# Overflow experts' weights asked for by halves and waited for one by one, and retention's first panels asked for after the gate/up products

## The reference, cut to what matters

```python
for i in range(DEPTH):                       # DEPTH = 4
    kind = i % 3                             # 0 attention, 1 pooling, 2 retention
    mp, ms = adaln(c_ctx, w_ada[i]), adaln(c, w_ada[i])
    x = x + gate * mixer[kind](modulate(rmsnorm(x)))
    x = x + gate * moe(modulate(rmsnorm(x)))

def moe(t):                                  # top-1 of 4 groups, top-2 of 4 experts in it
    hg = einsum('td,edf->tef', t, w_gate)    # (16 experts, 1024, 256)
    hu = einsum('td,edf->tef', t, w_up)      # (16 experts, 1024, 256)
    act = silu(hg) * hu * gates[:, :, None]
    return einsum('tef,efd->td', act, w_down)   # (16 experts, 256, 1024)

def retention(h):                            # layer 2 only
    p = h @ w_in                             # (1024, 6144): q, k, v, gate of 8 heads
```

## Time and profile before

| | |
|---|---|
| median of 3 executions | 1488.9 us (1486.45 to 1489.36) |
| the profiled execution | 1489.63 us |
| its span, first to last instruction | 1487.7 us |
| PE busy | 1390.4 us (93%) |
| DVE busy | 729.7 us (49%) |
| mean granted TensorE clock | 0.982 of full |
| mean DMA rate | 279 GB/s |

### The profile page before, as it was taken

One profiled execution on the slowest core, in us unless ns is written; L12 is line 12 of the kernel. 1 busy time (PEld: TensorE's weight loads), 2 busy tenths in 40 slices (PEclk: granted clock), 3 DMA queues, 4 the chain that ended last, 5 costly groups with the idle time before them and its releaser, 6 DMA issues. The chain is left out here.

```text
span 1487.7 us, 18189 instructions
## 1 busy us (share of the span) xinstructions
PE 1390.4 (93%) x6741; PEld 745.7 (50%) x6741; DVE 729.7 (49%) x1869; ACT 309.3 (21%) x697; POOL 92.2 (6%) x102
## 2 busy tenths in 40 slices
PE   5998898999699999899999999999996999999996
PEld 2334544544376443556666666446442446565442
DVE  1254303644527544666666666216542557146444
ACT  2104404110143100511111111013100305241111
POOL 0000011000220001000000000010000110110003
PEclk9999999999899999999999999999998999999998
DMA  9988976899678997745555555247999841047995
GB/s 381 401 325 350 420 284 269 345 424 416 255 287 333 418 423 272 269 127 176 182 183 172 167 172 209 84 199 286 405 422 404 329 179 64 6 165 294 423 423 204
DMA packets 122181, 414.56 MB, mean 279 GB/s; under 512 B 7184, under 2 KB 63344, under 8 KB 86512
## 3 DMA queue, kind: packets, MB, share of 16 engines
q1 hardware_dynamic: 106720, 374.92, 64.9%
q10 hardware_dynamic: 11920, 25.94, 4.5%
q0 software_dynamic: 3456, 12.58, 2.5%
HBM read 391.89 MB, written 21.53 MB: 278 GB/s over the span
## 5 line engine op out<-in xcount | busy, mean ns | idle before, releaser
L1234 PE MATMUL bank<-gate_up_weights,hT_gathered 128*64 128x512 f32 (+1 forms) x1280 | 256.5, 600 | 13.6 <-SPq L584 12.0
L1234 PEld LDWEIGHTS bank<-gate_up_weights,hT_gathered 128*64 128x64 f32 (+1 forms) x1280 | 82.5, 133 | 179.7 <-issue 179.7
L1045 PE MATMUL bank<-panel,hT 128*128 128x512 f32 x384 | 167.9, 597 | 4.1 <-DMA panel<-in_ret_w_in 3.2
L1248 PE MATMUL bank<-down_weights,actT 128*64 128x512 f32 (+1 forms) x640 | 131.5, 598 | 6.3 <-ACT actT L2627 6.3
L1764 DVE SCALAR_TENSOR_TENSOR ada_sums<-panel,cond_columns,ada_sums 128x384 f32<-128x384 f32 x224 | 121.1, 610 | 0.0
L1045 PEld LDWEIGHTS bank<-panel,hT 128*128 128x128 f32 x384 | 73.4, 192 | 93.4 <-issue 88.3
L1219 PE MATMUL bank<-P,h_hi 128*128 128x256 f32 x384 | 99.5, 296 | 0.0
L2615 ACT ACTIVATE silu<-bank 128x256 f32<-128x256 f32 x36 | 13.8, 383 | 390.4 <-PE bank L1234 390.4
L1219 PE MATMUL bank<-P,h_lo 128*128 128x256 f32 x384 | 94.2, 283 | 0.0
L699 PE MATMUL bank<-panel,oT 128*128 128x512 f32 x192 | 84.3, 595 | 1.3 <-ACT oT L2506 0.7
L1219 PEld LDWEIGHTS bank<-P,h_hi 128*128 128x128 f32 x384 | 73.3, 191 | 22.7 <-issue 22.7
(11 more groups left out here) (407 smaller groups left out, 1883.5 us busy)
## 6 DMA issues: line engine op xcount, KB each, us to landing
gate_up_weights<-in_gate_up_halves SPq DMA_DIRECT2D x134, 1024.0 KB, 14.1
down_weights<-in_down_rows SPq DMA_DIRECT2D x67, 1024.0 KB, 14.9
panel<-in_ada_panels SPq DMA_DIRECT2D x54, 1024.0 KB
panel<-in_w_ada SPq DMA_DIRECT2D x16, 1536.0 KB
ada_panel_third<-in_ada_panels SPq DMA_DIRECT2D x18, 1024.0 KB
y_by_slot<-y_rows ACTq DMA_DIRECT2D x32, 512.0 KB, 8.0
panel<-in_ret_w_in SPq DMA_DIRECT2D x16, 1024.0 KB
panel<-in_attn_w_qkv SPq DMA_DIRECT2D x5, 2048.0 KB
```

The lines of the kernel that those rows point to most:

```text
L1045: last = PE.matmul(ps[t][:], hT[:, k, t * 128:(t + 1) * 128], panel[f % 2][:, k, :], start=k == 0, stop=k == KD - 1)
L1234: last = PE.matmul(ps[2][width * s:width * s + width, :], hT_of(k)[:, width * s:width * s + width], gu_ring[w][:, 2 * k // KD, :, k % (KD ...
L1248: last = PE.matmul(ps[6 + half][width * s:width * s + width, :], actT[:, c, width * s:width * s + width], dn_ring[w][:, c, half * 512:half ...
```

## The change

Four things change. SP loads the last row's weights in a new function, `load_rest`, which takes the count of experts as a number: it first reads all experts' numbers, then asks for the first halves of all, the second halves of all, and the down weights of all. It is entered by one branch for two experts and by another for one; for that, DVE computes one more flag (`used == 1`, one tensor_scalar more in each layer) and SP reads it. PE then waits for `rest_gu0_landed`, `rest_gu1_landed` and `rest_dn_landed` directly, and SP no longer waits for any landing; if there is nothing to load, SP raises the three itself. Last, ahead of retention SP waits for the gate/up products of the passes (`o_gateup`; there are none here) and no longer for `quads_done`.

```diff
+    def load_rest(sp, l, n):
+        before = ROWS * l + PAIRS - 1
+        experts = [sp.value_load(unit_ids[0:1, l, i:i + 1], min_val=0, max_val=EXPERTS - 1) for i in range(n)]
+        for half in range(2):
+            sp.wait_ge(sem(("row_gateup_half", "row_gateup")[half]), before)
+            for i, e in enumerate(experts):
+                sp.dma_start(gu_ring[GU_OF[0][i]][:, half], at_e(gu_w[half], l, e).rearrange("p (a k f) -> p a k f", a=2, f=FE))\
+                    .then_inc(sem(f"rest_gu{half}_landed"), 32 // n)
+        sp.wait_ge(sem("row_down"), 2 * before)
+        for i, e in enumerate(experts):
+            sp.dma_start(dn_ring[DN_OF[0][i]][:], at_e(dn_w, l, e).rearrange("p (c n) -> p c n", n=D))\
+                .then_inc(sem("rest_dn_landed"), 32 // n)
...
                 sp.wait_ge(sem("row_gateup"), ROWS * l)
-                sp.wait_ge(sem("quads_done"), l)
+                if l == 2:
+                    atleast(sp, "o_gateup", sum(passes))
+                else:
+                    sp.wait_ge(sem("quads_done"), l)
...
-            for i in range(2):
-                with sp.If(used > i):
-                    e = sp.value_load(unit_ids[0:1, l, i:i + 1], min_val=0, max_val=EXPERTS - 1)
-                    for half in range(2):
-                        sp.wait_ge(sem(("row_gateup_half", "row_gateup")[half]), before)
-                        load_half(sp, l, e, GU_OF[0][i], half, f"quad_gu{l}_landed")
-                    sp.wait_ge(sem("row_down"), 2 * before)
-                    load_down(sp, l, e, DN_OF[0][i], f"quad_dn{l}_landed")
-            for i in (1, 0):
-                with sp.If(used > i):
-                    sp.wait_ge(sem(f"quad_gu{l}_landed"), 32 * (i + 1))
-            sp.sem_inc(sem("quad_ready"), 1)
-            for i in (1, 0):
-                with sp.If(used > i):
-                    sp.wait_ge(sem(f"quad_dn{l}_landed"), 16 * (i + 1))
-            sp.sem_inc(sem("quad_ready"), 1)
+            single = sp.value_load(extra[0:1, 2 * DEPTH + l:2 * DEPTH + l + 1], min_val=0, max_val=1)
+            with sp.If(used > 1):
+                load_rest(sp, l, 2)
+            with sp.If(single > 0):
+                load_rest(sp, l, 1)
+            with sp.If(used < 1):
+                for name in ("rest_gu0_landed", "rest_gu1_landed", "rest_dn_landed"):
+                    sp.sem_inc(sem(name), 32)
...
                 if last_row:
-                    pe.wait_ge(sem("quad_ready"), 2 * l + 1)
+                    pe.wait_ge(sem(f"rest_gu{2 * k // KD}_landed"), 32 * (l + 1))
...
         if last_row:
-            pe.wait_ge(sem("quad_ready"), 2 * l + 2)
+            pe.wait_ge(sem("rest_dn_landed"), 32 * (l + 1))
...
+            step(V.tensor_scalar(extra[:, 2 * DEPTH + l:2 * DEPTH + l + 1], incl[:, 15:16], 1.0, None, ALU.is_equal))
```

More of the change, by code:

```diff
@@ L160, in build_trunk @@
     rankm = keep("rank_in_expert", [TILES, EXPERTS])
-    extra = keep("more_quads", [2 * DEPTH], I32)
+    extra = keep("more_quads", [3 * DEPTH], I32)
     unit_ids = keep("unit_experts", [DEPTH, UNITS], I32)
@@ L566, in _ @@
                 load_row_down(sp, l, q, 2 * q, 2 * q + 1)
-            q = PAIRS
-            before = ROWS * l + q - 1
             sp.wait_ge(sem("units_known"), l + 1)
```

## The result

The changed kernel took 1480.8 us, the median of 5 runs (1478.37 to 1482.99), beside 1488.9 us (1486.45 to 1491.51) of the kernel before on the same chip: a ratio of 0.9948, with a 95% interval of 0.9933 to 0.9962. Unaltered, it was measured twice more beside its variants: 0.9958 (0.9944 to 0.9971) and 0.9971 (0.9961 to 0.9981). The mean of the three ratios is 0.9959, 6.1 us; the first measurement, 8.1 us, is the most favourable of them. The profiled execution has a span of 1481.0 us (before 1487.7) and took 1482.99 us.

A forecast was written before the change was run, and what follows sets the result against it. PE, busy 93% of the span, was read for its waits on loads. Gains of 6.9 (layer 2's sums), 0 (layer 3's overflow row) and 2.3 (retention's panels) sum to 9.2 us: 1488.9 to 1479.7 us, range 1476.0 to 1485.0.

The forecast's parts named there:

- rival 3: Retention's panels at the entry into layer 2 give nothing: 1482.0 to 1483.0 us; chance 0.17.
- The landings kept their slots: Layer 2's overflow row: six 1 MB loads keep their landing times, 1136.1 to 1149.7, when the order of requests changes.
- rival 5: Overflow row loads land in another order than asked for, wait not shortened: 1488.9 less 0 to 2.3 us; chance 0.05.
- Sums of layer 2, 6.9 us: DVE's overflow sums in layer 2 start at 1159.7 in place of 1166.6, gathers deciding; bounds 4.5 and 9.0 us.
- takes 0 to 2 do not move: gathers 0 to 2 hang on row 7's store: Layer 2: DVE's first three takes keep their times, number 2's gather landing at 1155.5; only gather 3 comes earlier.
- My lower bound of 4.5: Least gain at layer 2's sums, if layer 3's earlier panels hold take 3 up by 2.4 us.
- Retention's panels, 2.3 us: Entry into layer 2: panel lands 0.9 us earlier and first products save 1.45 us; bounds 3.8 and 0.
- so I charge nothing: Layer 1's gathers: tile 0's scaled input, up to 1.0 us later at 601.4, stays ahead of the panel at 601.9.
- the 1.6 us that I had named as what would make me wrong: Layer 1: the forecast fails if the panel's early packets slow the gathers by more than 1.6 us.
- 1.45 us for the 16 products: Entry into layer 2: at full clock the first 16 matmul records take 7.11 us in place of 8.56.
- The overflow row of layer 3, 0 us: PE's 1.55 us gain in layer 3's last row stays hidden behind the gathers; bounds 0 and 1.5 us.
- The rest, 0: DVE's additional flag, PE's waits and SP raising the semaphores itself cost nothing; bounds 0 and 0.8 us.

The follow-up runs named there:

- the overflow row alone: Changed kernel with retention's panels waiting for `quads_done` again, only the overflow row's part kept; against the kernel before: 1483.63 us, 0.9974.
- The panels alone: Kernel before with only retention's first panels asked for once layer 1's gate/up products are done, overflow row as before: 1486.22 us, 0.9985.
- with 20 matmuls: Changed kernel with 20 additional unused 16-column matmuls ahead of layer 1's pooling, moving PE's program; against the kernel before: 1485.32 us, 0.9976.
- the kernel before with 48 matmuls: Kernel before with 48 additional unused 16-column matmuls ahead of layer 1's pooling: 1499.73 us, 1.0066.
- the old order of requests: Changed kernel asking for the overflow row's weights expert by expert as before, PE still waiting for each half; against the kernel before: 1484.2 us, 0.9964.
- the version with one wait: Changed kernel, requests by halves, but PE waits for both halves before the overflow row's first product; against the kernel before: 1484.13 us, 0.9963.
- with the panels held back: Changed kernel with SP waiting for the previous layer's gather 3 to land before the panels of layers 2 and 3; against the kernel before: 1487.31 us, 0.9996.

## Why the prediction was right, and where its steps were wrong

The forecast was 1479.7 us (1476.0 to 1485.0), faster; measured 1480.8, and faster in all three measurements. Its sum of 9.2 us was too high: 8.1 in the first measurement, 6.1 over the three. That the forecast lies 1.1 us from the result is in part the luck of the first measurement: by the mean of the ratios the kernel is at 1482.8, still in the range, but where rival 3 (the panels give nothing: 1482.0 to 1483.0, chance 0.17) had put it.

- **The landings kept their slots** in the new order of requests. I had PE start 4.9 us behind R7, half 1 land at 10.6 and gate/up end at 14.2; it was 5.0, 10.6 and 14.3. The down weights cost nothing. Right, and the part on which rival 5 hung. In five profiles the second half takes 5.34 us, at a granted clock of 0.68 over it (3.64 us at 1.00 in the profile after), and gate/up ends at 16.0; the sums are not later for it (27.4 in the changed kernel's profile with it).
- **Sums of layer 2, 6.9 us: too high.** The term measured 4.0 in the profile after, 4.6 by the means of the profiles (40.2 - 35.6), and 3.9 (2.4 to 5.5) by the ratio of the overflow row alone, which takes in layer 3's row too. I had the sums 26.0 us behind R7; they came at 28.9, 27.4 and 28.6. The step that failed is "takes 0 to 2 do not move: gathers 0 to 2 hang on row 7's store". They do hang on it, and the store itself landed 1.3 to 1.5 us later, because PE's earlier start brought a q8 packet into it (begun at R7 + 9.1, before at R7 + 17.3). With the packet moved away, the sums came at 25.7 and 24.8, at or ahead of my figure. The rest is gather 3: I let it land 7.3 us behind its issue, 2.3 behind number 2, as in layer 1 before; in the changed kernel's profiles it took 7.4 to 8.6 us. My lower bound of 4.5, which stood for panels holding take 3 up, was the better estimate of the size; that it was the panels isn't shown here (7.2 us without them, 7.4 at best with them).
- **Retention's panels, 2.3 us: the size right, the working only in part.** The panels alone gave 2.2 us (0.7 to 3.7). I had the panel land 0.9 us earlier; it was from 0.4 to at least 0.9, and with 20 matmuls 0.7 later. The step that failed is the price for the gathers, "so I charge nothing": gather 3 of layer 1 took 9.3 us in place of 6.3, take 3 starts 1.6 to 2.7 us later behind the issue of gather 0, past the 1.6 us that I had named as what would make me wrong, and tile 0's input takes the panel's place. In the changed kernel the projection's start moved by 0.1 us in the mean: 21.8, 20.9 and 22.0 us behind gather 0, late panels 21.6 and 21.8. For this start rival 3 was right; for the gain it was not. What came back is the clock, as I had guessed with 1.45 us for the 16 products (8.56 before; 7.88, 7.11 and 7.94 after; granted clock over them 0.83 before; 0.90, 1.00 and 0.89 after), but mostly elsewhere: 8.9 or 7.25 us in retention's first head, which stood in no term of the sum. That the sizes agree is in part luck. From gather 0 to R7 it is 551.4 and 552.6 us with panels behind `quads_done`, 548.2 to 550.6 in the five profiles with early panels and the fast head, and 551.2 to 552.1 in the three with early panels, the slow head and PE's program unmoved. So nearly all of the gain lies in those profiles in which that clock stayed up. Whether the early panels bring that about, or five of ten beside none of four is chance, these runs don't settle, all the less as three of the five are of one kernel.
- **The length of one gap doesn't tell the clock here.** I had 3.21 us without work cost 1.45 us, and 1.55 us cost nothing. And I had taken the gap that would be left as 1.5 us; by the earlier trace rows it is 3.21 - 0.9 = 2.3 us, for which I had no row. With the panel's wait at 3.35 us the 16 products took 7.13 (granted clock over them 1.00), at 2.71 us 8.55 (0.83), at 5.04 us 9.51 (0.75), and without a wait of their own 7.88 (0.90) (8.56 behind 3.21, 0.83). The records of the granted clock in all 14 profiles hold the values 1.00 and 0.50 alone; what lies between is the mean of a stretch with both.
- **The overflow row of layer 3, 0 us: slightly low.** From gather 0's issue to the end it is 27.7, 28.0 and 28.2 us with the old row, and 26.6 to 27.5 in the ten profiles with halves waited for apart (mean 27.1): about 0.9, within my bound of 1.5. The chain that ends last is the one that I had named in 13 of the 14 profiles: it goes by gather 4, and with the old row that step took 6.25, 6.67 and 6.87 us, with the new one 5.2 to 6.2. The rest of the way from gather 0's issue to the end is 21.3 to 21.5 us in all thirteen, so the gain is gather 4's. Two lines of such chains, the longest (the kernel before with 48 matmuls) and one of the shortest (the old order of requests):

```profile
1477.59 6.87 DMA residual_term<-y_by_slot,slot_of_token
```

```profile
1461.90 5.22 DMA residual_term<-y_by_slot,slot_of_token
```

  So "None of that waits for the overflow row" held, and yet the row reached the end by way of the gathers. Why gather 4 is faster beside the new row stays open. The exception is the version with one wait: there the chain goes by PE, which stops for 2.53 us ahead of its last scatter products, runs them at a granted clock of 0.62, and ends at 29.2:

```profile
1464.94 8.02 PE L1294 MATMUL bank<-y_rows,logit_parts 128*128 128x512 f32 x11 [2.53 <-issue]
```

- **The rest, 0**: nothing in the profiles speaks against it; no run takes it by itself.

SP's panels do slow POOL's gathers, and the runs show it twice: with the early panels gather 3 of layer 1 took 9.3 us (6.8 with the panels held back), and a stream ahead of gather 0 of layer 2 took that one from 4.5 to 8.1. What rival 3 made of it, that nothing is gained by the panels, did not come true: alone they gave 2.2 us.

I had not thought of the instruction queue: with one q8 packet of 16 KB within it, row 7's store took 9.1 to 9.3 us in place of 7.8 to 7.9.

## What to carry to other kernels

When a wait is cut, read what stands just behind it: here 4.0 of 8.9 us arrived, in the profile after, and what held the rest was gathers whose start and landing both moved. List each of them with its own landing, and charge it with what the change puts beside it on the DMA engines. A load asked for some 3 us earlier landed 0.4 to about 1 us earlier here (DMA engines busy 0.89 and then 1.06 of the time), once 0.7 us later, and a gather of 512 KB beside it, number 3 of layer 1, took 9.3 us in place of 6.3. In layer 3, panels asked for 3 us earlier, ahead of the gathers, moved the entry from 33.8 to 38.1 us. For differences of 2 or 3 us read the same stretch from the same anchor in several profiles before believing one: the entry of one unaltered kernel varied by 2.9 us.

## What was not expected of the hardware

- In the changed kernel a packet of 16 KB of the instruction queue q8 took 1.06 us of one DMA engine's time. In all 14 profiles such a packet began when 5242 to 5266 of PE's matmul records had begun, from 14.9 us ahead of R7 to 17.3 us behind it. Row 7's store took 9.1 to 9.3 us in the seven profiles in which a q8 packet fell into it, and 7.8 to 7.9 in the seven without. The changed kernel has 50 such packets for 6741 matmuls and as many weight loads; that they are PE's program is my inference from these counts.
- The granted clock behind one and the same wait of 2.28 us was 1.00 in the changed kernel and 0.50 in the kernel before, and the place took 7.25 us or 8.9 in versions that differ elsewhere. Each version but the changed kernel has one profile, and its three agree, so how much of this is chance from one execution to the next isn't shown.
- PE stood still for 4.20 and 3.91 us with a q8 packet within that time, where the DMA engines were busy 1.06 and 1.00 of the time; before the change such a stop was 1.36 us, at the end of layer 3. In all eleven such stops (0.43 to 4.20 us) PE went on 1.4 to 1.8 us behind the end of a packet.
- A matmul of 16 columns in f32, two records, took 0.34 us where 48 of them stand (96 records in 16.2 us, granted clock 0.64; 0.50 from 406 to 414) and 0.27 where 20 do (40 records in 5.44 us, granted clock 0.81). So a record of 16 columns took 0.17 and 0.14 us, and one of 512 columns 0.44 at a granted clock of 1.00 (16 in 7.11): small ones were dear for their columns. How much of that is the clock isn't shown.
